# A decoder step: sample attention one sample deeper, a counting step moved to later head steps

## The reference

```python
def dsa_sample(q, k_new, v_new, iq, ik_new, iw, cache_k, cache_v, cache_ik, page_table, layer):
    ...
    sc = indexer_scores(iq, iw, ik_all)
    sc = jnp.where(adm[None], sc, -jnp.inf)
    _, idx = lax.top_k(sc, topk)
    ...
    k_sel = jnp.where(sel, cache_k[phys, layer, slot], k_new[bi, nidx])
    v_sel = jnp.where(sel, cache_v[phys, layer, slot], v_new[bi, nidx])
    return attend_selected(q, k_sel, v_sel, valid)
```

## Time and profile before

| what | us |
|---|---|
| median of 3 runs | 2015.89 |
| lowest, highest run | 2012.55, 2018.69 |
| the profiled execution | 2018.13 |
| its span in the profile | 2016.5 |
| busy in the span: PE, DVE, ACT, POOL | 1883.6, 872.2, 792.2, 655.5 |
| prompt attention in the span | 1462.9 to 1663.9 |
| sample attention | 1663.9 to 1758.2 |

### The profile page before, as it was taken

The page is one execution under the profiler, slowest core; times in us unless marked ns, Lnnn a source line. Parts: engine busy times, 40 slices in busy tenths (PEclk is TensorE's granted clock), DMA queues, the critical chain, the costliest instruction groups (busy, mean ns, idle before and its releaser), DMA issues. The chain is left out here.

```text
span 2016.5 us, 30755 instructions
## 1 busy us (share of the span) xinstructions
PE 1883.6 (93%) x10988; PEld 1656.3 (82%) x10988; DVE 872.2 (43%) x1646; ACT 792.2 (39%) x1148; POOL 655.5 (33%) x399
## 2 busy tenths in 40 slices
PE   7999999899999999999959989999979997799998
PEld 6999999899878888779958559999946764499997
DVE  4113334221124443142266867787786623521433
ACT  4234233222243333232144764677846553311311
POOL 4333333355333334645511221111122003245220
PEclk8999999999999999999979899999989998799999
DMA  6223222122222322331131110312231007241111
GB/s 183 74 64 84 73 73 81 55 83 84 85 80 85 89 87 84 94 95 32 31 132 40 30 55 22 97 32 82 80 108 30 1 1 245 98 141 42 43 54 45
DMA packets 226179, 150.75 MB, mean 75 GB/s; under 512 B 16755, under 2 KB 219251, under 8 KB 225715
## 3 DMA queue, kind: packets, MB, share of 16 engines
q1 hardware_dynamic: 210754, 125.78, 21.2%
q0 software_dynamic: 5152, 14.48, 2.4%
q10 hardware_dynamic: 10192, 9.46, 1.4%
HBM read 133.24 MB, written 16.43 MB: 74 GB/s over the span
## 5 line engine op out<-in xcount | busy, mean ns | idle before, releaser
L425 POOL TENSOR_TENSOR wlo<-wraw,whi 128x1024 fp32r<-128x1024 f32 x177 | 430.7, 2434 | 751.4 <-ACT whi L420 749.2
L437 PE MATMUL PS<-hhi_g,whi 128*128 128x288 f32 (+1 forms) x1152 | 324.8, 336 | 12.5 <-POOL wlo L425 7.2
L437 PE MATMUL PS<-hhi_g,wlo 128*128 128x288 f32 (+1 forms) x1152 | 317.3, 330 | 0.0
L437 PE MATMUL PS<-hlo_g,whi 128*128 128x288 f32 (+1 forms) x1152 | 317.2, 329 | 0.0
L420 ACT ACTIVATE whi<-wraw 128x1024 fp32r<-128x1024 f32 x177 | 186.5, 1054 | 327.1 <-PE PS L437 308.1
L437 PE MATMUL PS<-hhi,whi 128*128 128x364 f32 x1176 | 270.3, 338 | 23.5 <-DVE hlo L524 12.4
L437 PE MATMUL PS<-hlo,whi 128*128 128x364 f32 x1176 | 262.5, 332 | 0.0
L437 PE MATMUL PS<-hhi,wlo 128*128 128x364 f32 x1176 | 261.0, 330 | 0.0
L437 PEld LDWEIGHTS PS<-hhi,whi 128*128 128x128 f32 x1176 | 204.4, 191 | 31.4 <-issue 24.8
L437 PEld LDWEIGHTS PS<-hhi_g,whi 128*128 128x128 f32 x1152 | 196.1, 190 | 32.0 <-issue 6.9
L437 PEld LDWEIGHTS PS<-hhi_g,wlo 128*128 128x128 f32 x1152 | 196.5, 189 | 17.8
(11 more groups left out here) (378 smaller groups left out, 2764.5 us busy)
## 6 DMA issues: line engine op xcount, KB each, us to landing
wraw<-in_w_in_a_dram SPq DMA_DIRECT2D x96, 512.0 KB, 3.9
wraw<-in_w_out_a_dram SPq DMA_DIRECT2D x32, 512.0 KB, 3.9
wraw<-in_w_in_b_dram SPq DMA_DIRECT2D x25, 512.0 KB, 3.8
wraw<-in_w_pe_gate_dram SPq DMA_DIRECT2D x16, 512.0 KB, 4.0
kpg<-in_cache_k_dram SPq DMA_DIRECT2D x64, 128.0 KB, 2.5
vpg<-in_cache_v_dram POOLq DMA_DIRECT2D x64, 128.0 KB, 2.4
xs<-xT SPq DMA_DIRECT2D x1, 4368.0 KB, 12.6
xT<-xs SPq DMA_DIRECT2D x1, 4368.0 KB, 13.1
```

The costliest lines, as they stand in the source:

```text
L425: nc.gpsimd.tensor_tensor(wlo[par][:], wraw[par][:], whi[par][:].bitcast(F32), ALU.subtract).then_inc(w_lo, 1)
L437: mm = nc.tensor.matmul(o, w[par][:, k, :], r(k, c0, cn), start=first and i == 0 and n == 0, stop=last and i == KD - 1 and n == 2)
```

## The change

Five things change in the sample attention and one in the prompt attention.

- Logits of sample b go into bank b % 2 instead of always bank 0, its probabilities into one of two buffers (`old_probs`, `new_probs`), so a sample's logits may be computed while the probabilities of the one before are still in use.
- The logits of the 64 new keys are computed for all eight samples ahead (`new_key_logits`), copied once by ACT, and their maxima are taken once by DVE.
- PE's order becomes turn b, fold b - 1, logits b + 2, key pages b + 3, values b. ACT copies keys of sample b + 3 and then exponentiates sample b + 2. DVE scales sample b + 1, then does the output of b - 1 and the gate products, then the maximum of b + 2.
- ACT's key copy signals each of its two halves, and the turn waits only for the first.
- The gate products stand one round earlier and behind the copy into qT.
- `above` moves from steps 0 to 4 to steps 24 to 28, the sample's `resolve` from steps 5 to 12 to steps 32 to 39.

```diff
@@ -281,7 +281,14 @@
...
         rsb = pl("rsb", [P, REP, P])
-        heads, fold = rsb[:, 0], rsb[:, 1, 0:NS]
+        heads, fold, new_max = rsb[:, 0], rsb[:, 1, 0:NS], rsb[0:NS, 1, NS:NS + DEC_B]
+        new_logits = rdiag[0:NS].rearrange("p r q -> p (r q)")
+        def old_probs(b):
+            return Ps[:, b % 2 * BANK:(b % 2 + 1) * BANK]
+        def new_probs(b):
+            return rsb[0:NS, 2 + b % 2, 0:NS]
         pring = [swp, tq, sqt, rbc]
...
@@ -1213,25 +1220,33 @@
...
                 for g in range(NKV):
-                    last = nc.scalar.activation(kTb[:, g, :], PSF[:, (4 + 2 * g) * BANK:(6 + 2 * g) * BANK], ACT.Copy)
-                last.then_inc(sa["ke"], 1)
+                    nc.scalar.activation(kTb[:, g, :], PSF[:, (4 + 2 * g) * BANK:(6 + 2 * g) * BANK], ACT.Copy).then_inc(sa["ke"], 1)
+            def exponents(b):
+                act.wait_ge(sa["nb"], b + 1)
+                if b >= 2:
+                    act.wait_ge(sa["tr"], b - 1)
+                nc.scalar.activation(old_probs(b), PS[:, b % 2, :], ACT.Exp, bias=snb[:, b:b + 1], scale=qcol[:, b:b + 1],
+                                     accum_out=ssm[:, b:b + 1])
+                nc.scalar.activation(new_probs(b), new_logits[:, b * NS:(b + 1) * NS], ACT.Exp, bias=snb[0:NS, b:b + 1],
+                                     scale=qcol[0:NS, b:b + 1], accum_out=ssn[:, 0, b:b + 1]).then_inc(sa["ex"], 1)
             kT_evac(0)
+            act.wait_ge(sa["qc"], 3)
+            nc.scalar.activation(new_logits, PS[0:NS, 1, :], ACT.Copy).then_inc(sa["qc"], 1)
+            for b in range(2):
+                kT_evac(b + 1)
+                exponents(b)
             for b in range(DEC_B):
-                act.wait_ge(sa["nb"], b + 1)
-                if b:
-                    act.wait_ge(sa["tr"], b)
-                nc.scalar.activation(Ps[:, 0:BANK], PS[:, 0, :], ACT.Exp, bias=snb[:, b:b + 1], scale=qcol[:, b:b + 1],
-                                     accum_out=ssm[:, b:b + 1])
-                nc.scalar.activation(Ps[0:NS, BANK:BANK + NS], PS[0:NS, 1, 0:NS], ACT.Exp, bias=snb[0:NS, b:b + 1],
-                                     scale=qcol[0:NS, b:b + 1], accum_out=ssn[:, 0, b:b + 1]).then_inc(sa["ex"], 1)
-                if b + 1 < DEC_B:
-                    kT_evac(b + 1)
                 act.wait_ge(sa["tr"], b + 1)
...
                 nc.scalar.activation(PsT[0:NS, 8, :], PS[0:NS, 5, 0:NS], ACT.Copy).then_inc(sa["pt"], 1)
+                if b + 3 < DEC_B:
+                    kT_evac(b + 3)
+                if b + 2 < DEC_B:
+                    exponents(b + 2)
...
@@ -1803,10 +1818,10 @@
...
                     mask_and_max(n + 2)
-                if n < 5:
-                    above(n)
-                elif n < 13:
-                    resolve(SAMPLE, NBLK - 2, scs[:], Ps[0:NS, :], acc, n - 5)
+                if 0 <= n - 3 * NH < 5:
+                    above(n - 3 * NH)
+                elif 0 <= n - 4 * NH < 8:
+                    resolve(SAMPLE, NBLK - 2, scs[:], Ps[0:NS, :], acc, n - 4 * NH)
             inverse_sums(NGR - 1)
...
@@ -1819,9 +1834,10 @@
...
                 top = smx[:, 0, b:b + 1]
-                nc.vector.reduce_max(top, PSF[0:NS, 0:BANK + NS], axis=AX.X)
-                own.link(nc.vector.reduce_max(smx[:, 1, b:b + 1], PS[NS:P, 0, :], axis=AX.X))
+                nc.vector.reduce_max(top, PS[0:NS, b % 2, :], axis=AX.X)
+                own.link(nc.vector.reduce_max(smx[:, 1, b:b + 1], PS[NS:P, b % 2, :], axis=AX.X))
                 own.link(nc.vector.tensor_tensor(top, top, smx[:, 1, b:b + 1], ALU.max))
+                own.link(nc.vector.tensor_tensor(top, top, new_max[:, b:b + 1], ALU.max))
                 dve.wait_ge(sa["qc"], 2)
...
@@ -1838,26 +1854,33 @@
...
             nc.vector.tensor_tensor(fold, ident[:, 0:NS], ident[:, NS:P], ALU.add).then_inc(sa["pre"], 1)
-            sample_max(0)
-            for b in range(DEC_B):
+            def sample_norm(b):
                 dve.wait_ge(sa["ex"], b + 1)
-                total = ssn[:, 0, b:b + 1]
+                total, old, new = ssn[:, 0, b:b + 1], old_probs(b), new_probs(b)
                 nc.vector.tensor_copy(ssn[:, 1, b:b + 1], ssm[NS:P, b:b + 1])
...
                 own.link(nc.vector.reciprocal(srs[NS:P, b:b + 1], total))
-                nc.vector.tensor_scalar(Ps[:, 0:BANK], Ps[:, 0:BANK], srs[:, b:b + 1], None, ALU.mult)
-                nc.vector.tensor_scalar(Ps[0:NS, BANK:BANK + NS], Ps[0:NS, BANK:BANK + NS], srs[0:NS, b:b + 1], None,
-                                        ALU.mult).then_inc(sa["nr"], 1)
+                nc.vector.tensor_scalar(old, old, srs[:, b:b + 1], None, ALU.mult)
+                nc.vector.tensor_scalar(new, new, srs[0:NS, b:b + 1], None, ALU.mult).then_inc(sa["nr"], 1)
+            dve.wait_ge(sa["qc"], 4)
+            own.link(nc.vector.reduce_max(new_max, new_logits.rearrange("p (b n) -> p b n", n=NS), axis=AX.X))
+            sample_max(0)
+            sample_max(1)
+            sample_norm(0)
+            for b in range(DEC_B):
                 if b:
                     heads_copy(b - 1)
-                for f in range(2 * b - 4, 2 * b - 2) if 2 <= b < 6 else ():
-                    own.link(gate_z(f, slice(NS, TP)))
+                if b + 1 < DEC_B:
+                    sample_norm(b + 1)
                 if b:
                     sample_out(b - 1)
-                if b + 1 < DEC_B:
-                    sample_max(b + 1)
+                for f in range(2 * b - 2, 2 * b) if 1 <= b < 5 else ():
+                    own.link(gate_z(f, slice(NS, TP)))
+                if b + 2 < DEC_B:
+                    sample_max(b + 2)
             heads_copy(DEC_B - 1)
...
@@ -2369,9 +2392,9 @@
...
                 if b:
-                    pe.wait_ge(sa["ke"], b)
-                if b >= 2:
-                    pe.wait_ge(sa["pt"], b - 1)
+                    pe.wait_ge(sa["ke"], 2 * b)
+                if b >= 3:
+                    pe.wait_ge(sa["pt"], b - 2)
                 for g in range(NKV):
...
@@ -2379,27 +2402,36 @@
...
             def sample_logits(b):
-                pe.wait_ge(sa["ke"], b + 1)
-                if b:
-                    pe.wait_ge(sa["ex"], b)
-                halves = [PS[NS * q:NS * q + NS, 0, :] for q in range(2)]
+                pe.wait_ge(sa["ke"], 2 * b + 2)
+                if b == 1:
+                    pe.wait_ge(sa["qc"], 4)
+                if b >= 2:
+                    pe.wait_ge(sa["ex"], b - 1)
+                halves = [PS[NS * q:NS * q + NS, b % 2, :] for q in range(2)]
                 keep = scs[:].bitcast(BF16)
...
                 for q in range(2):
-                    nc.tensor.matmul(halves[q], repb[:, b, :], keep[:, q * BANK:(q + 1) * BANK], start=False, stop=True)
-                for g in range(NKV):
-                    nc.tensor.matmul(PS[0:NS, 1, 0:NS], qb[:, b, g, :], kT[:, g, 0:NS], start=g == 0, stop=False)
-                nc.tensor.matmul(PS[0:NS, 1, 0:NS], repb[:, b, :], keep[:, PAST:SLS], start=False,
-                                 stop=True).then_inc(sa["s"], 1)
+                    mm = nc.tensor.matmul(halves[q], repb[:, b, :], keep[:, q * BANK:(q + 1) * BANK], start=False, stop=True)
+                mm.then_inc(sa["s"], 1)
+            def new_key_logits():
+                for b in range(DEC_B):
+                    out = PS[0:NS, 1, b * NS:(b + 1) * NS]
+                    for g in range(NKV):
+                        nc.tensor.matmul(out, qb[:, b, g, :], kT[:, g, 0:NS], start=g == 0, stop=False)
+                    mm = nc.tensor.matmul(out, repb[:, b, :], scs[:].bitcast(BF16)[:, PAST:SLS], start=False, stop=True)
+                mm.then_inc(sa["qc"], 1)
...
                 pe.wait_ge(sa["nr"], b + 1)
-                pe.wait_ge(sa["ke"], min(b + 2, DEC_B))
+                pe.wait_ge(sa["ke"], min(2 * b + 5, 2 * DEC_B))
+                if b:
+                    pe.wait_ge(sa["pt"], b)
                 for j in range(NPAGE // 2):
-                    nc.tensor.transpose(PS[:, 4, j * P:(j + 1) * P], Ps[:, j * P:(j + 1) * P], ident[:])
-                nc.tensor.transpose(PS[0:NS, 5, 0:NS], Ps[0:NS, BANK:BANK + NS], ident[0:NS, 0:NS]).then_inc(sa["tr"], 1)
+                    nc.tensor.transpose(PS[:, 4, j * P:(j + 1) * P], old_probs(b)[:, j * P:(j + 1) * P], ident[:])
+                nc.tensor.transpose(PS[0:NS, 5, 0:NS], new_probs(b), ident[0:NS, 0:NS]).then_inc(sa["tr"], 1)
...
@@ -2427,16 +2459,18 @@
...
             pe.wait_ge(sa["qc"], 2)
-            sample_logits(0)
-            k_pages(1)
+            new_key_logits()
+            for b in range(2):
+                sample_logits(b)
+                k_pages(b + 1)
             for b in range(DEC_B):
...
                     fold_halves(b - 1)
-                if b + 1 < DEC_B:
-                    sample_logits(b + 1)
                 if b + 2 < DEC_B:
-                    k_pages(b + 2)
+                    sample_logits(b + 2)
```

(2 more changed lines are left out.)

## The result

| what | before | after |
|---|---|---|
| median, us | 2016.26 (4 runs) | 1993.78 (4 runs) |
| lowest, highest run | 2012.55, 2018.69 | 1992.59, 1995.19 |
| the profiled execution | 2018.13 | 1995.19 |
| start of the prompt attention | 1462.90 | 1463.74 |
| prompt attention | 200.95 | 191.7 |

The ratio is 0.9889, 95% interval 0.9876 to 0.9901: 22.5 us faster, where 25.3 us were forecast. The two profiled executions differ by 22.9 us: 9.3 in the prompt attention, 14.5 in the sample attention, less 0.8 that the part before both took longer. The code ahead of the prompt attention is the same in all kernels of this document, and yet its start lies between 1459.8 and 1467.7 us in their traces; so of a difference between two executions some microseconds can lie outside the edit, and the stages are compared one by one.

What follows compares the result with a forecast made beforehand. Bounds taken: DVE at the start of the prompt attention, a ring of PE, ACT and DVE in the sample attention. 12.0 + 13.3 = 25.3 us off 2018.13 gives 1992.8, less 2.2 to the median: 1990.6 us; range 1983 to 2003.

Steps and rivals of the forecast that it cites:

- the ring of the samples: Sample attention: no engine full, PE, ACT and DVE wait on each other, 10.75 us per sample; opening it saves 13.3 us.
- First stretch: Prompt attention, head steps 0 to some 16: moving 13.0 us of DVE work out makes it 13.1 us shorter, 21.5 us.
- what the moved work costs later: Prompt attention, steps 24 to 39: PE nearly hides the moved DVE work; 1.1 us lost, bounds 0 and 6 us.
- rival A: Prompt attention, steps 24 to 39: moved DVE work is not hidden, 6 us comes back instead of 1.1; 1995.5 us, chance 0.10.
- no more than a microsecond longer: Sign for steps 24 to 31 and 32 to 39: neither group grows by more than a microsecond.
- First turn: Sample attention: PE's turn of sample 0 comes 7.7 us later, at 1683.9 instead of 1676.2.
- The open ring: Sample attention after the first turn: DVE's work, 8.0 us with gate products, 5.5 without; turns mostly 7 to 8 us apart.
- B: Sample attention: ring closes again behind ACT, clock dips, turns 10 us apart; 10.5 us saved instead of 13.3; 1993.4 us, chance 0.14.
- E: Sample turns stay 10.7 us apart and moved prompt work comes back; 7.1 us off or less, 2009 to 2012 us, chance 0.05.
- The end set by the value pages: Sample attention: POOL's 40 value-page issues at 1.17 us each set the end, 1744.9 instead of 1758.2, 13.3 us off.
- Rival C: Sample attention: value pages do not limit, as issue gaps shrink or start sooner; turns set the end; 1983.9 us, chance 0.10.
- Rival D: Sample attention: DVE holds POOL's issue queue; from 1.82 us per page the kernel is slower, at 1.95 it is 2021; chance 0.03.

## Why the prediction was right, point by point

**The time and both gains.** 1993.8 us against 1990.6. Both places, the start of the prompt attention and the ring of the samples, gave what they gave by the mechanism forecast. In the profiled executions the prompt attention gained 2.7 us less than forecast, by one term, and the sample attention 1.2 us more. That the two misses partly cancel is luck.

**First stretch.** Forecast 13.1 us off and 21.5 us long; it took 22.00. The mask of step 24 stands 37.3 us behind the first, 50.3 before: 13.0. DVE's busy time in the first sixteen steps went from 28.92 to 16.18 us.

**The mis-sized term: what the moved work costs later.** Forecast 1.1 us, measured 3.7 over the whole prompt attention: 3.6 in steps 24 to 31 and 0.8 in steps 32 to 39, less 0.7 that the steps behind gave back. Two things failed in the step. I looked for the trouble in the heavy tie resolution of steps 32 to 39; that cost 0.8 there and, with what the steps behind gave back, 0.2 in all. (DVE was busy 21.14 us there, not 23: the last parts of the tie resolution fall into steps 40 to 47.) And I compared DVE's work with the length of the stretch (18.0 of 19.14 us, measured 18.12) and asked only for the masks, with one step in hand. The path that broke was a longer one: a late inverse of the row sums on DVE, GpSimd's 1.58 us diagonal, PE's sum. It was 2.1 us late, once, and 1.3 us went to the clock. With the counting step eight steps later it cost 0.2 us. This is rival A at some three fifths of its size (6 us), and the sign "no more than a microsecond longer" failed in steps 24 to 31.

**First turn.** Forecast 7.7 us later, measured 6.1 (18.5 us behind the stage's start, 12.4 before). I had given the logits of sample 1 the slow 3.24 us of the earlier trace rows; they took 1.94, and those of sample 2 took 3.56, behind the first turn. The eight new-key groups took 4.15 us, forecast 4.1.

**The open ring.** Turns at 1673.92, 1681.78, 1688.35, 1696.08, 1703.65, 1711.28 and 1716.95: 7.9, 6.6, 7.7, 7.6, 7.6 and 5.7 us apart; forecast 7.8, 6.8, 7.9, 7.9, 7.9 and 5.9. The eighth turn came another 7.2 us later, at 1724.10, forecast 4.3: sample 6's values had waited 3.3 us for their pages. DVE's loop was taken as the limit of the rounds with gate products, and the run with the later fold bears it out. Rivals B and E are gone with these distances.

**The end set by the value pages.** 40 issues over 45.9 us, 1.18 each against 1.17 assumed; the stage is 14.5 us shorter, forecast 13.3, by the earlier first turn. One of the two sources of the 1.17 was misread: SyncE did not issue its 40 key pages without stopping in the trace before. Twice, at the first page of a sample, which waits for its buffer, 2.6 and 2.7 us lie between two starts there. In the changed kernel, without such stops, the same 40 take from 1658.3 to 1701.6, 1.11 each and not 1.19. GpSimd's own 0.54 + 0.62 was the right row. Rival C is refuted as it was put (no gap shrank, and turns did not set the end), but sixteen pages on another queue gave 9.0 us more, so the time that it named was there to be had. Rival D needed 1.82 us a page. By the rule of the Trainium skill, "SBUF — State Buffer", section "Who interferes with whom", some issues would be held; of the 40 one did take longer, 0.631 us against a median of 0.536, and it began within 0.02 us of DVE's scaling of `Ps` (L1865, 0.49 us). So the trace agrees with the rule, at a price of 0.1 us in the whole stage. The forecast had this rule from the issue of 0.81 us and named its neighbour wrongly: L1645, 0.77 us long, compares the sample's scores with the threshold and scales no mask. Nor was it the only one: another issue of the trace before took 0.82 us beside L1654, which does scale the mask.

## What to carry to other kernels

Work on an engine with room on the average goes into a stretch for free only if no hand-over of that stretch passes through it late: follow every chain that starts on that engine, also the rare one through a third engine, and compare the place with ones where the covering engine has more work. After a ring is opened, count the issues of each queue that feeds it; a queue that kept pace with the old ring can become the end of the new one. Here moving a part of it to another queue was worth 9.0 us and tightening the loop nothing. One trace has one history of the clock: compare a stretch over several executions before a microsecond in it is put down to an edit.

## What the runs showed of the hardware

- The same 2.1 us stop of TensorE at the same instruction was followed by the lower clock in three executions and by the full clock in two; it made a stretch of 21.47 us into one of 22.65 to 22.75.
- A page issue takes 0.33 us on SyncE and 0.54 us on GpSimd, but with the page's number read from the table the pace is nearly one: SyncE's 16 value pages started over 16.8 us, 1.12 each, GpSimd's 40 over 45.9, 1.18 each. What fills the 0.6 to 0.8 us between was not tried.
- The unchanged sample attention took 94.4 us at a mean clock of 0.82 and 96.7 us at 0.78 in two executions of the same instructions; the one with the open ring took 79.5 to 79.9 in five of the six kernels that had it unedited, and 78.1 in the sixth.
- Of GpSimd's 40 page issues in the sample attention the one that began with DVE's scaling of `Ps` took 0.631 us instead of 0.536; in the trace before, during the prompt attention, two took 0.81 and 0.82 us beside DVE instructions of 0.77 and 0.71 us on 64 rows of 1088.
